# A decoder layer on one core: the first modulation quarter split into two eighths, and three column groups begun together

## The reference, cut to what matters

```python
mod = jax.nn.silu(c) @ w_ada[l] + b_ada[l]              # c: 2048, w_ada: 2048 x 12288
sh_m, sc_m, ga_m, sh_f, sc_f, ga_f = jnp.split(mod[:, None, :], N_MOD, axis=-1)
h = rmsnorm(x, g_pre_mix[l]) * (1.0 + sc_m) + sh_m
y = token_mixer(h, cos, sin, lb_all[l], w_in[l], ...)   # first of all h @ w_in
x = x + ga_m * rmsnorm(y, g_post_mix[l])
h = rmsnorm(x, g_pre_ffn[l]) * (1.0 + sc_f) + sh_f
y = swiglu(h, w_gate_up[l], w_down[l])
x = x + ga_f * rmsnorm(y, g_post_ffn[l])
```

## Time and profile before

| | |
|---|---|
| median of 3 runs | 1864.67 us (1864.29 to 1865.28) |
| the profiled execution's own time | 1865.72 us |
| span of its profile | 1863.9 us |
| PE busy | 1820.3 us, 98% of the span |
| DVE busy | 1296.5 us, 70% |
| ACT busy | 893.6 us, 48% |
| moved from HBM | 420.36 MB |

### The profile page before, as it was taken

How to read it: one execution, slowest core, us unless ns; L and a number is a source line. 1 busy time by engine, 2 the same in 40 slices (tenths; PEclk the granted TensorE clock), 3 DMA queues, 4 the chain that set the end, 5 groups by cost and what they waited for, 6 DMA issues and landing times. The chain is left out here.

```text
span 1863.9 us, 24368 instructions
## 1 busy us (share of the span) xinstructions
PE 1820.3 (98%) x8828; PEld 1529.1 (82%) x8828; DVE 1296.5 (70%) x1373; ACT 893.6 (48%) x1023; POOL 105.1 (6%) x74
## 2 busy tenths in 40 slices
PE   3999999999999999999999999999999999999998
PEld 3878888888888888888888878888888888888886
DVE  6889768677677677678787555656666666665657
ACT  5544555645645645654334456443443443443343
POOL 0000000130130130120000000000000000000000
PEclk8999999999999999999999999999999999999999
DMA  9997657656656656647787646666666666665553
GB/s 359 400 383 271 197 168 276 231 173 225 225 174 221 231 173 222 200 153 256 274 327 239 225 159 203 215 232 224 204 232 228 210 224 224 225 213 174 195 187 133
DMA packets 115986, 423.38 MB, mean 227 GB/s; under 512 B 13009, under 2 KB 13393, under 8 KB 115409
## 3 DMA queue, kind: packets, MB, share of 16 engines
q1 hardware_dynamic: 115920, 422.51, 66.3%
HBM read 420.36 MB, written 2.10 MB: 227 GB/s over the span
## 5 line engine op out<-in xcount | busy, mean ns | idle before, releaser
L1320 DVE TENSOR_TENSOR wlo<-raw,whi 128x1024 fp32r<-128x1024 f32 x600 | 731.6, 1222 | 398.4 <-ACT whi L484 397.4
L484 ACT ACTIVATE whi<-raw 128x1024 fp32r<-128x1024 f32 x600 | 629.7, 1053 | 712.1 <-PE PS L898 653.2
L890 PE MATMUL PS<-whi,hT_hi 128*128 128x512 f32 x1760 | 694.4, 395 | 4.1 <-issue 3.0
L891 PE MATMUL PS<-whi,hT_lo 128*128 128x512 f32 x1760 | 686.5, 390 | 0.0
L898 PE MATMUL PS<-wlo,hT_hi 128*128 128x512 f32 x1760 | 471.5, 390 | 0.0
L890 PEld LDWEIGHTS PS<-whi,hT_hi 128*128 128x128 f32 x1760 | 331.2, 188 | 71.7 <-issue 3.3
L898 PEld LDWEIGHTS PS<-wlo,hT_hi 128*128 128x128 f32 x1760 | 330.9, 188 | 69.6
L891 PEld LDWEIGHTS PS<-whi,hT_lo 128*128 128x128 f32 x1760 | 331.3, 188 | 66.5 <-issue 0.2
L890 PE MATMUL PS<-whi,cT_hi 128*128 128x512 f32 (+1 forms) x592 | 229.1, 389 | 0.0
L891 PE MATMUL PS<-whi,cT_lo 128*128 128x512 f32 (+1 forms) x592 | 226.1, 384 | 0.0
L1327 DVE SCALAR_TENSOR_TENSOR ada_acc<-ada_raw,csilu,ada_acc 128x512 f32<-128x512 f32 (+1 forms) x185 | 141.2, 763 | 27.8 <-DMA ada_raw<-in_ada 24.0
(11 more groups left out here) (238 smaller groups left out, 1112.4 us busy)
## 6 DMA issues: line engine op xcount, KB each, us to landing
ada_raw<-in_ada SPq DMA_DIRECT2D x142, 512.0 KB, 4.8
raw<-in_w_gate SPq DMA_DIRECT2D x88, 512.0 KB, 4.2
raw<-in_w_up SPq DMA_DIRECT2D x88, 512.0 KB, 4.1
raw<-in_w_down SPq DMA_DIRECT2D x88, 512.0 KB, 4.2
raw<-in_w_start SPq DMA_DIRECT2D x80, 512.0 KB, 4.8
raw<-in_w_hf SPq DMA_DIRECT2D x32, 512.0 KB, 3.7
raw<-in_w_hq SPq DMA_DIRECT2D x32, 512.0 KB, 5.0
raw<-in_w_hi SPq DMA_DIRECT2D x32, 512.0 KB, 4.4
```

The lines of the kernel that those rows point to most:

```text
L484: nc.scalar.activation(whi[:, pl.slot(c), 0:w], raw[:, pl.slot(c), 0:w], ACT.Copy)\
L890: nc.tensor.matmul(o, hi[:, kt, tok], whi[:, s, cols], start=c == 0 and k == 0, stop=False)
L891: nc.tensor.matmul(o, lo[:, kt, tok], whi[:, s, cols], start=False, stop=False)
L1320: nc.vector.tensor_tensor(wlo[:, s, 0:w], raw[:, s, 0:w], whi[:, s, 0:w].bitcast(F32), ALU.subtract)\
```

## The change: what it does

- The sixteen chunks of the first modulation quarter are cut anew: chunks 0 to 7 hold the columns of channels 0 to 255 (the first eighth), each for two blocks of 128 rows of w_ada, and chunks 8 to 15 those of channels 256 to 511. VectorE takes such a chunk in two halves of 512 columns, each added to the same sum (`eighth_chunk`). Chunks 1 and 3 are not VectorE's: TensorE multiplies them by silu(c) itself, in banks 4 to 7 (`shared_chunk`), and the sum of the first eighth is added to that.
- The first three column groups are multiplied together: first the chunk of rows 0 to 255 of all three, then the chunk of rows 256 to 511 of all three. The third takes the banks from XB on. The weights in HBM are put in this order.
- The order of SyncE, ScalarE, TensorE and VectorE up to the sixth weight chunk is written anew; the scaling of x is split in parts of 512 and 1536 columns, and the eight transposes are spread between the sums and the first tiles.
- `ADA_PACE` is changed, and SyncE keeps three modulation chunks ahead throughout. TensorE sums the second quarter after group j = 8 in place of 6, before chunk 18; VectorE, ScalarE and VectorE make its scale, rows and low halves at c = 19 in place of 16, 17 and 18.
- Behind the start phase, TensorE's modulation sums go from step 39 to the end of step 38, and `ADA_LEAD` is one step earlier.

```diff
 ADA_FIRST = 3
-ADA_PACE = [(0, 0), (15, 16), (20, 21), (35, 32), (55, 48), (80, 48)]
+ADA_SHARED = [1, 3]
+N_E = 3
+ADA_PACE = [(0, 0), (3, 2), (19, 16), (20, 17), (35, 32), (55, 48), (80, 48)]
...
-                if a >= ADA_SLOTS:
-                    sp.wait_ge(ada_step, a - ADA_SLOTS + 1)
+                before = a - ADA_SLOTS
+                if before in ADA_SHARED:
+                    sp.wait_ge(sig("shared_step"), shared_before(before) + 1)
+                elif before >= 0:
+                    sp.wait_ge(ada_step, steps_before(before) + 1)
...
-            for a in range(KD):
+            for a in range(ADA_SLOTS):
                 load_ada0(a)
...
             start = place_c()
-            for c in range(RING):
+            for c in range(N_E):
                 load(start, c, w_start[c])
+            for a in range(ADA_SLOTS, KD):
+                load_ada0(a)
+            load(start, N_E, w_start[N_E])
             asked = KD + ADA_FIRST
             for a in range(KD, asked):
                 load_ada0(a)
...
-                    ahead = KD + ada_due(c - RING + 1) + min(ADA_SLOTS, ADA_FIRST + (c - RING) // 3)
-                    for a in range(asked, min(ahead, ADA0)):
+                    ahead = KD + ada_due(c - RING + 1) + ADA_FIRST
+                    for a in range(asked, min(ahead, ADA_ALL)):
                         load_ada0(a)
-                    asked = max(asked, min(ahead, ADA0))
+                    asked = max(asked, min(ahead, ADA_ALL))
...
             for tt in range(TT):
-                nc.scalar.activation(yb[:, tt], yb[:, tt], ACT.Copy, scale=stat[:, tt:tt + 1])\
-                  .then_inc(sig("x_scaled"), 1)
-            for kp in range(KD // 2):
-                act.wait_ge(sig("x_transposed"), kp + 1)
-                nc.scalar.activation(xT[:, kp], PS[:, kp % 4, :], ACT.Copy).then_inc(sig("xT_copied"), 1)
+                scale_x(tt, slice(0, NW))
+            scale_x(0, slice(NW, D))
+            copy_xT(0)
+            copy_xT(1)
+            scale_x(1, slice(NW, D))
...
             high(pl, 0)
+            scale_rows(1, 0, 1)
             high(pl, 1)
-            scale_quarter(0)
+            copy_xT(2)
+            copy_xT(3)
+            high(pl, 2)
+            copy_xT(4)
+            copy_xT(5)
+            high(pl, N_E)
+            scale_rows(2, 1, 2)
+            copy_xT(6)
             for c in range(N_C + AHEAD):
-                if c > 1:
+                if c > N_E:
                     high(pl, c)
+                if c == 2 * N_E:
+                    copy_xT(7)
                 n, i = divmod(c, SG * W_G)
-                if i == 17 and n < PH - 1:
-                    scale_quarter(n + 1)
-                j, odd = divmod(c - AHEAD, W_G)
-                if odd == W_G - 1 and 0 <= j < SG:
-
-                    from_pair(pl, j, c - AHEAD, start_sum[j])
+                for q, at in ((1, SG * W_G - 1), (2, 2 * SG * W_G - 3), (3, 3 * SG * W_G - 3)):
+                    if c == at:
+                        scale_rows(q + 2, q * KP_Q, (q + 1) * KP_Q)
+                for j in range(SG):
+                    if c - AHEAD == start_tile(j, W_G - 1):
+
+                        from_pair(pl, j, c - AHEAD, start_sum[j], bank=XB if j == N_E - 1 else None)
...
-            pe.wait_ge(sig("constants_loaded"), 16)
-
-            pe.wait_ge(sig("x_scaled"), TT)
-            pe.wait_ge(ada_step, ADA_SLOTS)
-            for kp in range(KD // 2):
-                if kp >= 4:
-
-                    pe.wait_ge(sig("xT_copied"), kp - 3)
-                transpose_pair(yb, kp, kp % 4).then_inc(sig("x_transposed"), 1)
...
+            def shared_chunk(a):
+
+                slot = ada0_slot[a % ADA_SLOTS]
+                pe.wait_ge(ada_loaded[a % ADA_SLOTS], (a // ADA_SLOTS + 1) * 16)
+                for i in range(2):
+                    for j in range(HPG):
+                        last = nc.tensor.matmul(PS[:, XA + j, 0:1], slot[:, i * NW + j * P:][:, 0:P],
+                                                csilu[:, 2 * a + i:2 * a + i + 1], start=a == ADA_SHARED[0] and i == 0, stop=False)
+                last.then_inc(sig("shared_step"), 1)
+
+            def sum_first_eighth():
+
+                pe.wait_ge(ada_step, steps_before(E_N))
+                for j in range(HPG):
+                    last = nc.tensor.matmul(PS[:, XA + j, 0:1], quarter_sum[0][:, j * P:(j + 1) * P], ones[:, 0:1],
+                                            start=False, stop=True)
...
-            sum_quarter(0)
-            pe.wait_ge(sig("xT_copied"), KD // 2)
+            pe.wait_ge(sig("c_silu"), 1)
+            for a in ADA_SHARED:
+                shared_chunk(a)
+            pe.wait_ge(sig("constants_loaded"), 16)
+            pe.wait_ge(sig("x_scaled"), TT)
+            transpose_x(0)
+            transpose_x(1)
+            sum_first_eighth()
+            pe.wait_ge(sig("x_scaled"), 2 * TT)
+            transpose_x(2)
+            transpose_x(3)
+            pe.wait_ge(sig("xT_copied"), 2)
+            first_tile(0, 0)
+            transpose_x(4)
+            pe.wait_ge(sig("xT_copied"), 4)
+            first_tile(1, 0)
+            transpose_x(5)
+            first_tile(2, 0)
+            sum_second_eighth()
+            transpose_x(6)
+            first_tile(0, 1)
+            first_tile(1, 1)
+            transpose_x(7)
+            first_tile(2, 1)
             for n in range(PH):
-                for j in range(SG):
+                for j in range(0 if n else N_E, SG):
                     for i in range(W_G):
                         if j == 0:
                             pe.wait_ge(sig("h_low"), n * KP_Q + i + 1)
                         multiply(pl, n * SG + j, W_G, (n * SG + j) * W_G, i, i + 1, hT_hi, hT_lo, kt0=n * W_G * KC)
-                    if j == 6 and n < PH - 1:
+                    if j == (6 if n else 8) and n < PH - 1:
                         sum_quarter(n + 1)
                     if n == PH - 1:
                         if j == 3:
@@ -1101,15 +1198,14 @@
                 if t == 35:
                     pe.wait_ge(sig("p_copied"), g * 2 + 2)
                     attend().then_inc(sig("att_summed"), 1)
-                if t == 39:
+                if t == 38:
+                    pe.wait_ge(sig("att_scaled"), g + 1)
+                    pe.wait_ge(pair_free[pl.pair(I_HF)], pl.freed(I_HF) + 1)
...
+            def eighth_scale(e):
+
+                src = PS[:, XA, HPG:2 * HPG].rearrange("p (a k) -> p a k", a=2) if e else                     PS[:, XA:XA + HPG, 0].rearrange("p (a k) -> p a k", a=2)
...
+            def rows_low_start(first, end):
...
+            def eighth_chunk(a):
+
+                e, b = divmod(a, E_N)
+                slot, acc = ada0_slot[a % ADA_SLOTS], quarter_sum[0][:, e * NW:(e + 1) * NW]
+                dve.wait_ge(ada_loaded[a % ADA_SLOTS], (a // ADA_SLOTS + 1) * 16)
+                for i in range(2):
+                    k = 2 * b + i
+                    if i:
+                        dve.wait_ge(sig("ada_half"), steps_before(a) + 1)
+                    elif b:
+                        dve.wait_ge(ada_step, steps_before(a))
+                    part = slot[:, i * NW:(i + 1) * NW]
+                    if k == 0:
+                        last = nc.vector.tensor_scalar(acc, part, csilu[:, 0:1], None, ALU.mult)
+                    else:
+                        last = nc.vector.scalar_tensor_tensor(out=acc, in0=part, scalar=csilu[:, k:k + 1], in1=acc,
+                                                              op0=ALU.mult, op1=ALU.add)
+                    last.then_inc(ada_step if i else sig("ada_half"), 1)
...
+            for a in range(E_N):
+                if a not in ADA_SHARED:
+                    eighth_chunk(a)
                 if a == 2:
 
                     dve.wait_ge(sig("x_squared"), TT)
                     nc.vector.tensor_scalar(stat[:, 0:TT], stat[:, 0:TT], 1.0 / D, EPS, ALU.mult, ALU.add)\
                       .then_inc(sig("trunk_mean"), 1)
+            second = [a for a in range(E_N, KD) if a not in ADA_SHARED]
+            eighth_chunk(second[0])
+            eighth_scale(0)
             low(pl, 0)
-            shift_and_scale(0)
-            quarter_low(0)
+            rows_low_start(0, 1)
+            eighth_chunk(second[1])
+            low(pl, 1)
+            eighth_chunk(second[2])
+            low(pl, 2)
+            for a in second[3:]:
+                eighth_chunk(a)
+            eighth_scale(1)
+            rows_low_start(1, 2)
+            low(pl, N_E)
...
-                if i == 16 and n < PH - 1:
-                    shift_and_scale(n + 1)
-                if i == 18 and n < PH - 1:
-                    quarter_low(n + 1)
+                    if a not in ADA_SHARED:
+                        ada0_chunk(a)
+                for q, at in ((1, SG * W_G - 1), (2, 2 * SG * W_G - 4), (3, 3 * SG * W_G - 4)):
+                    if c == at:
+                        quarter_scale(q)
```

(60 more changed lines are left out.)

60 lines of the change are left out of this document (36 added, 24 removed).

## The result

| | before | after |
|---|---|---|
| median | 1864.29 us (1863.24 to 1865.37, 7 runs) | 1870.95 us (1869.93 to 1872.14, 7 runs) |
| own time of the profiled execution | 1865.72 us | 1872.14 us |
| its span | 1863.9 us | 1870.4 us |

The changed kernel is slower: ratio 1.0036, 95% interval 1.0026 to 1.0045, that is 6.7 us in the medians and 6.4 to 6.5 in the profiled executions. The forecast was 1865.0 with a range of 1861.5 to 1868.5. One execution each of the later runs e2, e5 and e7 took 3.1 to 10.6 ms and is left out of their ratios.

A forecast was written before the change was run, and what follows sets the result against it. It took the first rows' readiness and, from about 100 to 140 us, VectorE's pace as the bound; -5.2 + 2.4 + 0.5 + 0.8 + 0.5 + 1.2 = +0.2 us gave 1865.0 us after the median correction, range 1861.5 to 1868.5.

The forecast's parts named there:

- Steps 1 to 3: Start: scale at 24.8, first weight matmul at 28.2, c = 3 at 45.3 against 50.46, a lead of 5.2 us.
- Step 4: TensorE's gap before c = 3: the clock falls again and costs 2.4 us, leaving a lead of 2.8.
- Step 5: Up to c = 6: a transpose step costs 0.5 us, the wait for bank pair 1 0.8; lead 1.5.
- Step 6: Seam at c = 20: group 8's banks cost another 0.5 us; c = 20 at 97.5 against 98.5, lead 1.0.
- Step 7: c = 20 to the third quarter's sum: VectorE's full queue takes 41.8 us, sum at 138.6, 0.2 later than before.
- The sum: All terms to the third sum: -1.0 us at c = 20, then +1.2 on the way to 138.6, making +0.2.
- Rival C: Behind c = 3 and at c = 6 or 20: low clock costs 6.3 us in place of 2.4; 1868.8, chance 0.08.
- The last line of the sum: From profiled execution to median: 1865.9 less 1.05 us gives 1864.9, say 1865.0.
- Edits at nothing: Steps 38 and 39, `ADA_LEAD`, and three modulation chunks ahead on SyncE: same instructions or enough cover, priced at no cost.
- step 1: First eighth: scale at 24.8, with TensorE's two shared chunks, transposes and half sum adding nothing to the path.

The follow-up runs named there:

- e2: Kernel before with only the modulation sums moved from step 39 to the end of step 38 and the lead pieces one step earlier; 1864.34 us, ratio 1.0000.
- e5: Kernel before with 64 one-element matmuls more at TensorE's very start; 1866.02 us, ratio 1.0008.
- e7: Kernel after with the old `ADA_PACE` and 48 one-element matmuls ahead of the loop; 1865.36 us, ratio 1.0003.
- e6: Kernel after with 48 one-element matmuls more ahead of the loop; 1868.12 us, ratio 1.0020.
- e13: Kernel after, own pace, with 32 one-element matmuls and TensorE multiplying through its wait for the second eighth; 1866.13 us, ratio 1.0010.
- e1: Kernel after with the modulation sums back in step 39 and `ADA_LEAD` as before; 1877.00 us, ratio 1.0062.
- e3: Kernel before with 16 one-column matmuls, results unread, at TensorE's idle start; 1872.33 us, ratio 1.0043.
- e4: Kernel after with the old `ADA_PACE`; 1868.76 us, ratio 1.0025.
- e8: e7 with ScalarE emptying group 1's banks before `high(7)` and group 8's before the second quarter's rows; 1864.57 us, ratio 1.0000.
- e10: e7 with the second quarter's sum after group 6, its scale, rows and low halves at c = 16 to 18, and group 1 emptied early; 1867.39 us.
- e14: e13 with a mixed pace: 2 chunks by c = 3, 21 by c = 20, then the old pace; 1867.18 us, ratio 1.0014.
- e12: e10 with TensorE multiplying through its wait for the second eighth, and 32 small matmuls in place of 48; 1868.84 us.

## Why the prediction was wrong, by its own steps

- **Steps 1 to 3** (scale 24.8, first matmul 28.2, c = 3 at 45.3): measured 25.43, 28.21 and 45.37. Right but for the scale: TensorE's part was not off its path, VectorE waited 0.78 us for the sum of the first eighth, and this cost the first matmul nothing. The lead of 5.2 us at c = 3 is 5.1 against the profile of the kernel before, and 3.5 against e2's.
- **Step 4** (the clock falls in the gap, 2.4): it fell (the first eight matmuls of c = 3 took from 45.37 to 48.95). From c = 3 to c = 6 it took 11.8 us; less three chunks of 2.72, the transposes' 0.5 and the wait of 0.69, 2.4 are left. The price was 2.0 in the medians (e6 to e13). The Trainium skill, TensorE: Matmul & The Clock Gate, section "HAM oscillation — how this bites in real kernels", has bursts parted by waits pay for the warm-up each time; the low clock behind the gap here, behind the turns of e1 and e3, and its absence in e13 agree; waits of 1.10 to 1.20 us before c = 20 in e4, e7 and e8 had no low clock behind them (1.00 from 97 to 107 us).
- **Step 5** (wait before c = 6 of 0.8, lead 1.5): 0.69, and c = 6 at 57.16 against 58.62 before, lead 1.46 against that profile (in e2 c = 6 started at 57.02, which leaves none). Right by its own rows, and e8 and e10 show that group 1's copy is the cause.
- **Step 6** (c = 20 at 97.5): 97.59, with a wait of 0.20 in place of 0.5. Right.
- **Step 7** (third sum at 138.6): 139.05, 0.45 late; VectorE is busy for 25.00 of 25 us as said, and the wait of 1.26 is VectorE's. The sum of this step was right in kind and 0.45 short. It starts at `low(20)` (96.7, measured 96.62), and so a lead at `low(20)` passes through to the third sum, and so does a delay: e13 has `low(20)` 1.78 us sooner than e6 and the third sum 1.83 sooner. What takes the lead back is the length of the stretch, with its four products more, and not a time before which the third sum can't come, as the expectation of e13 had it.
- **The sum** left out what follows a wait in VectorE's full stretch: the clock fell behind it, 1.56 us. Rival C had a wait lower the clock once more, but at c = 6 or 20 and for 1.2; it was right in kind, in the wrong place.
- **The last line of the sum** took 1.05 us off, because the median of the kernel before lies that much under its profiled execution. Nothing showed that the changed kernel would get this back. In e2 the kernel before is ahead by its clock at the start (third sum at 136.56 in place of 138.39), where VectorE holds the changed kernel's at about 139 in all three profiles. So the forecast third sum of 138.6 was 0.2 us late only against a slow start of the kernel before, and 2.0 late against e2.
- **The step that failed is a term put at nothing.** "Edits at nothing" weighed the moves inside the stretch behind 265 us and found the same instructions there. They are the same (e2: 1864.34); but the 16 matmuls of the shared chunks, which step 1 priced at nothing by their time, shift the place of everything behind them, and the loop's turns then wait for instructions: 4.19 us in the profile, 2.8 in the medians of after and e6, 8 in e3. No row that was read before pointed there, and no rival had it.

By medians, undoing the place of the loop is worth 2.8, undoing the pace 2.2 (the third sum and the low clock behind it), and both together 5.6 of the 6.7 (e6, e4, e7).

## What to carry to other kernels

Price an edit also by what its instructions displace: when a kernel has a loop, read the instruction queue's row (packets in all, and within the loop's turns) before and after, and add or remove a few small instructions ahead of the loop before believing any difference in it. A lead that is won by emptying the engine that binds must be followed to each place where a sum or a scale waits, because a wait of a microsecond can cost more than a second one in the clock (1.26 and then 1.56 in after; 1.10 and then nothing in e4). Compare one program place once per turn: it showed within a few lines that 4.2 of the 6.4 us between the two profiles (2.8 of 6.7 by medians) were lost 250 us behind the change. And take a second profile of the kernel before: here its start alone differed by 1.8 us between two executions, where the forecast added up to 0.2.

## What the runs showed of the hardware that was not expected

- A loop of TensorE that takes 139 us a turn runs either with one 16 KB transfer of instructions from 487 to 780 us or with 18 or 19. It was 18 or 19 in after, e1, e3 and e4, and 1 in before, e2 and e5 to e14; the program's length ahead of the loop decides, and not in one direction (16 matmuls more: refetch; 64 more: none). What the period is and how much the engine holds was not tried.
- What a refetch costs differs from program to program: 4.2 us over two turns in after, 3.1 in e4, 7.9 in e3 and 10.0 in e1 (each against 138.96 and 138.98). In e1 and e3 each turn's wait was in one piece (1.5 to 2.3 us), and the clock fell behind it: its mean over the 8 us around each was 0.59 and 0.63 in e1, 0.79 and 0.64 in e3.
- The same wait (1.25 us) and the same sum of one-column matmuls (1.95 us) were followed by a fall of the clock in after and e6, and not in e13's profile. The times of e13 reach from 1864.56 to 1867.66, which would fit a fall in some executions and not in others; this is argued, not shown. In e12 a wait of only 0.58 us before the same kind of sum was followed by a fall (0.79 from 82 to 90 us).
- The low clock at a kernel's start differs between executions with the same start: in before's profile it was 0.50 from 40 to 44 us, in e2's 0.71, and TensorE was 1.6 us ahead at c = 3.
